# Decoder layer on one core: another order of the heads at the boundaries of the attention blocks

## What is computed

```python
def block(args):                      # 128 query rows, 8 heads, latent keys of width 128
    ...
    iscore = jnp.einsum('bths,bth->bts', rel, wi_b.astype(jnp.float32))
    _, sel = lax.top_k(iscore, topk)  # 256 keys per query row
    ...
    logits = jnp.einsum('bthc,btkc->bthk', ql_b, kv_sel).astype(jnp.float32)
    probs = jax.nn.softmax(logits, axis=-1).astype(kv_sel.dtype)
    return jnp.einsum('bthk,btkc->bthc', probs, kv_sel)
...
mix = jnp.concatenate([y_ret, y_dsa], axis=-1) @ w_out[i]
x = x + rms_norm(mix, post_mix_g[i])
f = rms_norm(x, pre_ffn_g[i])         # then a gated FFN, and a gated embedding
```

## Time and profile before

| | us |
|---|---|
| median of 3 runs | 1504.99 |
| the runs | 1502.03 to 1505.8 |
| the profiled execution, its own time | 1505.4 |
| its span in the trace | 1503.7 |
| attention stage in the span | 476 to 736 |

### The profile page before, as it was taken

The page is one execution under the profiler, slowest core; times in us unless marked ns, Lnnn a source line. Parts: engine busy times, 40 slices in busy tenths (PEclk is TensorE's granted clock), DMA queues, the critical chain, the costliest instruction groups (busy, mean ns, idle before and its releaser), DMA issues.

```text
span 1503.7 us, 19694 instructions
## 1 busy us (share of the span) xinstructions
PE 1435.3 (95%) x7125; PEld 1176.4 (78%) x7125; DVE 1082.8 (72%) x1566; ACT 630.4 (42%) x1229; POOL 311.0 (21%) x378
## 2 busy tenths in 40 slices
PE   7999999999798789999899999999999999999998
PEld 7887888887686557777677888888887888888886
DVE  5749988999888768884387777777776676557543
ACT  5444443218525656657353222222223455544212
POOL 3544457503610344433100000000000000000000
PEclk9999999999999999999999999999999999999999
DMA  6322233317133111112214444444446976663111
GB/s 204 78 54 78 79 95 111 99 54 258 30 126 119 42 43 43 57 43 71 83 44 160 163 164 162 164 164 164 164 164 240 323 242 228 228 224 112 57 56 43
DMA packets 138256, 189.30 MB, mean 126 GB/s; under 512 B 13872, under 2 KB 76720, under 8 KB 138160
## 3 DMA queue, kind: packets, MB, share of 16 engines
q1 hardware_dynamic: 121328, 152.44, 31.4%
q10 hardware_dynamic: 16832, 35.61, 6.2%
HBM read 130.34 MB, written 57.67 MB: 125 GB/s over the span
## 4 chain that ended last, share of the span: by engine, by line
PE 72%; DVE 8%; issue 5%; ACT 5%; DVEq 4%; DMA 3%; POOL 2%; SPq 0%; ACTq 0%; POOLq 0%
PE ps L705 19%; PE ps L706 19%; PE ps L707 19%; PE ps L979 4%; DVEq L1876 3%; DVE sc L1860 2%; PE ps L914 2%; DVEq L1874 2%; PE ps L905 1%; DMA rb<-in_w_ffn_down 1%; DVE m L1873 1%; PE ps L877 1%; DVE lm L2011 1%; ACT pt L1423 1%; PE ps L833 1%
## 5 line engine op out<-in xcount | busy, mean ns | idle before, releaser
L1873 DVE MAX8 m<-sc 128x8 f32<-128x640 f32 (+5 forms) x176 | 162.2, 921 | 10.4 <-issue 2.0
L2446 POOL TENSOR_TENSOR smf<-smf,sml 128x1 f32<-128x1 f32 x16 | 9.1, 579 | 742.4 <-DVE smf L2327 628.4
L1875 DVE MATCH_REPLACE8 sc<-m,sc 128x640 f32<-128x640 f32 (+5 forms) x176 | 159.6, 907 | 0.8 <-issue 0.6
L705 PE MATMUL ps<-bh,ah 128*128 128x512 f32 x308 | 120.3, 390 | 0.1
L707 PE MATMUL ps<-bh,al 128*128 128x512 f32 x308 | 120.0, 390 | 0.0
L706 PE MATMUL ps<-bl,ah 128*128 128x512 f32 x308 | 120.0, 390 | 0.0
L705 PE MATMUL ps<-wbh,xth 128*128 128x512 f32 (+1 forms) x320 | 119.4, 373 | 0.0
L706 PE MATMUL ps<-wbl,xth 128*128 128x512 f32 (+1 forms) x320 | 118.5, 370 | 0.0
L707 PE MATMUL ps<-wbh,xtl 128*128 128x512 f32 (+1 forms) x320 | 118.4, 370 | 0.0
L2271 DVE TENSOR_TENSOR al<-ra,ah 128x512 fp32r<-128x512 f32 x77 | 53.2, 691 | 78.0 <-ACT ah L1616 77.8
L705 PE MATMUL ps<-th,ssh 128*128 128x512 f32 x240 | 93.7, 390 | 1.8 <-DVE u2b L2155 1.2
(11 more groups left out here) (319 smaller groups left out, 3762.4 us busy)
## 6 DMA issues: line engine op xcount, KB each, us to landing
raw<-in_w_in SPq DMA_DIRECT2D x49, 256.0 KB, 3.0
wt<-in_w_ffn_down SPq DMA_DIRECT2D x44, 256.0 KB, 7.0
down_sums<-wt ACTq DMA_DIRECT2D x44, 256.0 KB, 5.0
ra<-hidden_sums SPq DMA_DIRECT2D x44, 256.0 KB, 2.9
rb<-down_sums SPq DMA_DIRECT2D x44, 256.0 KB, 4.0
raws<-in_w_ffn_gate SPq DMA_DIRECT2D x21, 512.0 KB, 4.1
raws<-in_w_ffn_up SPq DMA_DIRECT2D x21, 512.0 KB, 5.4
ret_rows<-stg SPq DMA_DIRECT2D x32, 320.0 KB, 3.6
```

The lines of the kernel that those rows point to most:

```text
L705: pe.matmul(o, ah, wh, start=start, stop=False, skip_group_check=resumes)
L1873: v.max(M8[:, :], sc_b)
L1875: v.match_replace(sc_b, M8[:, :], sc_b, PICKED)
```

## The change

At each block boundary (T = 8b + 14, where the projection of block b runs) TensorE's queue is put in another order. Before: logits(T), projection, values(T-3), transposes(T-2), [step T+1] logits(T+1), transposes(T-1), values(T-2), head values, [step T+2] logits(T+2) and so on. After: logits(T), transposes(T-2), values(T-3), first half of the projection, logits(T+1), second half, [step T+1] logits(T+2), transposes(T-1), values(T-2), head values, [step T+2] transposes(T), values(T-1). A half is the eight matmuls of one output half; before, the halves alternated.

ScalarE copies the projection in step T+1 instead of T, behind the exponent, and squares the mix in step T+2 instead of T+1 (not for the last block).

LATE's default goes from 5 to 6: the square over the residual rows and the transposes of the FFN rows of blocks 0 to 5 come one head step later. Their copy on ScalarE goes one step further, in front of the copy of the probabilities, and in that step TensorE puts the values ahead of the transposes.

```diff
-        return next((b for b in range(RT) if t == b * H + H - 1 + lag + LATE.get(b, 5)), None)
+        return next((b for b in range(RT) if t == b * H + H - 1 + lag + LATE.get(b, 6)), None)
...
     for t in range(STEPS + TAIL):
+        if 2 <= t <= STEPS + 1:
+            tp_use.append(("tr", t - 2))
         if at_block(t, 7) is not None:
             tp_use.append(("mx", at_block(t, 7)))
-        if 2 <= t <= STEPS + 1:
-            tp_use.append(("tr", t - 2))
...
-        def out_projection(b):
-
-            tp_free(("mx", b))
-            pe.wait_ge(s["a_ms"], ms_read(ms_at[("yt", b)])[0] + 1)
-            if b == 0:
-                pe.wait_ge(s["load_wo"], 32)
+        def out_projection(b, dh):
+            if dh == 0:
+                tp_free(("mx", b))
+                pe.wait_ge(s["a_ms"], ms_read(ms_at[("yt", b)])[0] + 1)
+                if b == 0:
+                    pe.wait_ge(s["load_wo"], 32)
+            ds = slice(dh * 512, (dh + 1) * 512)
             for k in range(NP):
-                for dh in range(2):
-                    m = pe.matmul(pair(2)[:, dh * 512:(dh + 1) * 512], YDT[:, k, :],
-                                  WO[:, k, dh * 512:(dh + 1) * 512], start=(k == 0), stop=(k == NP - 1))
-            m.then_inc(s["t_tp"], 1)
+                m = pe.matmul(pair(2)[:, ds], YDT[:, k, :], WO[:, k, ds], start=(k == 0), stop=(k == NP - 1))
+            if dh == 1:
+                m.then_inc(s["t_tp"], 1)
...
         for t in range(STEPS + TAIL):
-            if t < STEPS:
+            if t < STEPS and at_block(t - 1, 7) is None and at_block(t - 2, 7) is None:
                 logits(t)
-            if at_block(t, 7) is not None:
-                out_projection(at_block(t, 7))
-                if 3 <= t <= STEPS + 2:
-                    prob_values(t - 3)
+            if t + 1 < STEPS and at_block(t - 1, 7) is not None:
+                logits(t + 1)
+            values_first = at_late(t - 1, FT_LAG) is not None
+            if values_first and 3 <= t <= STEPS + 2:
+                prob_values(t - 3)
             if 2 <= t <= STEPS + 1:
                 prob_transposes(t - 2)
-            if 3 <= t <= STEPS + 2 and at_block(t, 7) is None:
+            if not values_first and 3 <= t <= STEPS + 2:
                 prob_values(t - 3)
...
+            if at_block(t, 7) is not None:
+                out_projection(at_block(t, 7), 0)
+                if t + 1 < STEPS:
+                    logits(t + 1)
+                out_projection(at_block(t, 7), 1)
...
         for t in range(STEPS + TAIL):
-            if at_block(t, 8) is not None:
-                mix_square(at_block(t, 8))
+            if at_block(t, 9) not in (None, RT - 1):
+                mix_square(at_block(t, 9))
+            if at_block(t, 8) == RT - 1:
+                mix_square(RT - 1)
...
             if 1 <= t <= STEPS:
                 exponent(t - 1)
-            if at_block(t, 7) is not None:
-                read_mix(at_block(t, 7))
+            if at_block(t, 8) not in (None, RT - 1):
+                read_mix(at_block(t, 8))
+            if at_late(t - 1, FT_LAG) is not None and at_late(t - 1, FT_LAG) < RT - 1:
+                read_ffn_rows(at_late(t - 1, FT_LAG))
+            if at_block(t, 7) == RT - 1:
+                read_mix(RT - 1)
             if 2 <= t <= STEPS + 1:
                 read_probs(t - 2)
...
-            if at_late(t, FT_LAG) is not None:
-                read_ffn_rows(at_late(t, FT_LAG))
+            if at_late(t, FT_LAG) == RT - 1:
+                read_ffn_rows(RT - 1)
```

## The result

The changed kernel takes **1498.04 us** (median of 6 runs, 1495.66 to 1498.78) against 1505.0 us before on the same chip, a ratio of 0.995 with the 95% interval 0.9937 to 0.9962. The forecast was 1490.6 us with the range 1486 to 1499, and 87% for a gain over 0.3%. The sign is right and the time lies in the range, at its upper end, but the gain of 7.0 us is half of the 14.8 that were forecast.

The account below looks back on a forecast made before the run. VectorE sets the pace between boundaries; at each, TensorE's order makes it wait. Boundary gains of 16.9 us, +0.4 at T = 62 and +1.7 for the clock give -14.8, from 1505.4 to 1490.6 us; range 1486 to 1499.

Parts of the forecast that it names:

- The 9.0 us before the projection: TensorE's waits for the transposed y ahead of the projection: nearly all of the 9.0 us were to go.
- the logits between the halves: At T = 38, logits T+1 ready at 590.7, before VectorE asks at 594.3; VectorE's wait of 2.99 us vanishes.
- both slow stretches: Half-clock stretches in the projections behind 552 and 586 us, 1.7 us each; one counted as coming back.
- Two signs that the prediction named: Right if masks of T+1 carry no wait on the logits' line; wrong if a mask waits on the transposes' line.
- The place of the copy of y: On ScalarE, with the square one head later, the y copy ends some 1.06 us earlier at T = 38.
- +0.4: Last boundary, T = 62: gate and up weights land late, last values end 0.4 us later; bounds +0.4 and -2.1.
- in front of exponent T-1, which nobody needs until the projection ends: Place of the residual-row square on ScalarE at T; at T = 38 the projection's 1.30 us wait goes.
- the mask of T+2: It waits for transposes of T-1, these for the projection's copy; logits T+2 cover 0.9 us, TensorE waits some 0.2.
- T = 54: Boundary of block 5's projection: gain of 2.0 us, the smaller of 2.34 and 2.7 - 0.7.
- the square over the mix: At T+2 on ScalarE, waiting for GpSimd's sum: no loss at T = 38, 1.0 and 0.5 us at T = 14 and 22.
- The rival that gave ScalarE's queue 17%: Mix square's wait not absorbed: half of its 2.37 us on the path at six boundaries, 1497.8 us; chance 17%.
- one of two stretches as coming back: Clock at the projections of T = 30 and 38: one of two half-clock stretches stays, +1.7 us on the sum.

Follow-up runs that it names:

- e2: The changed kernel with SyncE issuing the first gate and up weight loads earlier, ahead of its wait for block 5's rows; 1496.76 us.
- e1: The changed kernel with ScalarE copying the probabilities of T-2 ahead of the square and exponent T-1 at step T; 1494.8 us.
- e3: The changed kernel with the edits of e1 and e2 together; 1489.45 us.
- e9: e3 with ScalarE copying the projection in two halves of 512 columns, the first while the second half runs (last block's copy whole); 1486.9 us.
- e4: e3 with ScalarE's square over the mix at T+2 behind the copy of the probabilities of T, not ahead of exponent T+1; 1490.89 us.
- e5: The changed kernel with the logits of T+1 behind both halves of the projection instead of between them; 1500.22 us.

## Why the prediction was right, and where it was too large

**Right.** The 9.0 us before the projection went; the logits between the halves came before VectorE asked at T = 38, 46 and 54; both slow stretches of the earlier trace rows are not in the profile after; the blocks shrank, though by 1.45 to 2.03 us instead of 2 to 4. Two signs that the prediction named spoke against it: the masks of T+1 still wait for logits at the first three boundaries, and those of T+2 wait on the transposes' line. The place of the copy of y was right too: it ended at 579.5, long before it was needed. At T = 62 the chain was as forecast: the second load is issued 1.07 us behind the start of the projection (690.67) instead of 0.81 ahead of it, lands 6.4 us later, and ScalarE stands in front of its first cast with exponent 62 and the copy of the mix queued behind. Counted from the start of the projection, I had both the issue and ScalarE's arrival 3.2 and 3.5 us later; the difference, ScalarE's wait, was 6.1 by my numbers and 6.55 here.

```profile
691.74 0.57 SPq L592 DMA_DIRECT2D wrf<-in_w_ffn_up  x1
...
698.17 1.05 ACT L1540 CAST wh<-wrf 128x1024 fp32r<-128x1024 f32 x1 [6.55 <-DMA wrf<-in_w_ffn_up]
...
701.31 1.64 PE L905 MATMUL ps<-tab,lm 128*128 128x128 f32 x8 [2.57 <-ACT mxa L1449]
```

TensorE waits 2.57 us (forecast 3.5). From step 61 to the projection of T = 70 the lead fell by 1.2 us, of which 1.7 are a slow stretch, so +0.4 was forecast and -0.5 measured; in e2, with the weights in time, the lead rose by 1.4 (bound of the forecast: 2.1).

**The step that failed** is the sentence that the square runs "in front of exponent T-1, which nobody needs until the projection ends". Nobody needs the exponent, but the copy of the probabilities T-2 is queued behind it, and in the new order the projection needs that copy: transposes of T-2 now write the PSUM pair ahead of it. In the old order it was the copy of T-3, one step older. It stands in the first lines of the diff, where the use ("tr", t - 2) goes ahead of ("mx", ...) in the list that every wait for that pair is counted from. I had read these lines as bookkeeping. I listed what the moved transposes need, not what the projection must wait for once they are ahead. Price by e1 and e3: 5.7 us of the stage up to T = 62, 4.9 of the lead at step 61.

**Mis-sized: the mask of T+2.** "TensorE waits some 0.2" was 0.75, 0.64, 0.47 and 0.42 at T = 14 to 38, and I let VectorE's side of it be covered everywhere because it was at T = 38. At the first three boundaries it was not: 2.45, 1.72 and 2.13. Taking half of the copy off the path gave 1.7 us of lead (e9), a value between 0.2 per boundary and the whole wait, since the rest is the projection's own length.

**Mis-sized: T = 54.** Forecast 2.0, measured 0 (1.1 in e9). VectorE is 2.16 us ahead behind that boundary (10.70 at step 55) and has lost it by step 61, in e9 as well (16.99 at step 57, 15.06 at step 61). From the projection of T = 54 to that of T = 62 TensorE was busy for 37.52 of 37.88 us before. I had taken its idle time of block 6 as free to give, but most of it was the one wait at T = 54, and behind it there was no slack in which VectorE's lead could be kept.

**Rightly sized: the square over the mix.** I took 1.0 and 0.5 us for it at T = 14 and 22; moving it off the path gave 1.5 up to T = 62 (e4), though 0.5, 0.8 and 0.2 at the first three boundaries. The rival that gave ScalarE's queue 17% and 1497.8 us hit the measured time by luck, with the wrong mechanism: it named the wait for the sum, and it was the copy of T-2.

In sum the lead at step 61 was forecast as 16.9 and came out as 8.5. The copy's place explains 4.9 (of this 1.0 arises at T = 38, and most of it is the meeting of VectorE and GpSimd told below, which e3 does not have), the copy of the mix 1.7. With these two mended the kernel stands at 15.1 (e9). Of the 1.8 still missing, 0.9 lie at T = 54 and 0.6 at T = 22 (2.9 of 3.5); for the latter I have no cause.

**The clock.** I counted one of two stretches as coming back; both went, and one came at T = 62, so the count was right by luck and the place was not. The Trainium skill, "TensorE: Matmul & The Clock Gate", section "HAM oscillation", has the clock fall over waits between bursts of matmuls; its example spends about 1.67 us at the half rate per wait, of which half is the loss. The trace differs in size: a slow stretch of this stage is 3.4 us long and costs 1.7. All ten stretches between 476 and 736 us, in nine kernels, begin within 1.3 us of the end of a wait (0.95 to 5.13 us long). But most waits of these lengths have none behind them: at T = 62 TensorE waits 2.57 us in after and 2.37 in e5, with a slow stretch behind the one and a whole clock behind the other. So in this stage the rule names where such a stretch can come, not whether.

## What to carry to other kernels

When an operation is moved ahead of another that uses the same buffer, ask what the second must now wait for, not only what the first one needs: the release of the buffer moves with it, and whoever frees it must be early in its own queue. Work that is moved away was also cover for what followed it; look what waited 0.2 us behind it. And two mends on one chain can be worth more together than their sum, so a small gain of one alone (1.3 us) is no reason to leave it out.

## What the runs showed of the hardware

- In the profiles of 14 kernels the half clock costs between 6.3 and 11.9 us up to 1484 us of the span, most of it at places that no edit touched. A difference of 1 to 2 us between two spans can be one such stretch; it was told apart here only by stretches with the granted clock.
- VectorE's two subtractions of line 1994 take 1.38 or 1.39 us for the other blocks and 2.21 at T = 38 of after, where they ran beside GpSimd's scaling of the FFN rows, which itself took 1.54 instead of 1.12 us:

```profile
581.49 2.21 DVE L1994 TENSOR_TENSOR qst<-aq,qst 64x512 fp32r<-64x512 f32 x2
...
581.63 1.54 POOL L2598 TENSOR_SCALAR fn<-fn,sml 128x1024 f32<-128x1024 f32 x1
```

  In the kernel before the same pair met at T = 22; there GpSimd started first and kept its 1.12 us:

```profile
522.19 1.12 POOL L2586 TENSOR_SCALAR fn<-fn,sml 128x1024 f32<-128x1024 f32 x1
522.32 2.23 DVE L1982 TENSOR_TENSOR qst<-aq,qst 64x512 fp32r<-64x512 f32 x2
```

  The 0.8 us are part of what T = 38 fell short (2.0 against 3.2): in e3 and e9, where the two do not meet, the subtractions take 1.39 us and T = 38 gives 3.0. The Trainium skill, "SBUF — State Buffer", section "SBUF: two separate sides", says that a VectorE operation with two SBUF inputs and a GpSimd operation that reads SBUF share a pair of ports, which the one that starts first keeps for the whole instruction while the other is held up. Both pairs agree with that: in before only VectorE, which started second, is longer, by 0.8 us; in after the first subtraction (0.68 us) started first, the scaling became longer by 0.4 and the second subtraction, now behind it, by 0.8. I had put that scaling's new place down as free.
